# The last token pieces before a layer norm multiplied token tile by token tile, and GpSimd's weight half moved behind the norm's powers

## What is computed

```python
x = layer_norm(ALPHA * x + 0.5 * swiglu(x, ffn1_wg, ffn1_wu, ffn1_wd), ln1_g, ln1_b)
...   # S5, RG-LRU and RWKV-7 branches of x @ w_in, gated and summed into merged
x = layer_norm(ALPHA * x + merged @ mix_w_out, ln2_g, ln2_b)
x = layer_norm(ALPHA * x + cross_attention(x, mem, xa_wq, xa_wkv, xa_wo), ln3_g, ln3_b)
x = layer_norm(ALPHA * x + 0.5 * swiglu(x, ffn2_wg, ffn2_wu, ffn2_wd), ln4_g, ln4_b)

def layer_norm(x, g, b):
    mu = jnp.mean(x, -1, keepdims=True)
    var = jnp.mean(jnp.square(x - mu), -1, keepdims=True)
    return (x - mu) * lax.rsqrt(var + LN_EPS) * g + b
```

## Time and profile before

| what | us |
|---|---|
| median of 3 runs (1621.33 to 1622.28) | 1622.28 |
| the profiled execution, its own time | 1621.9 |
| its span | 1620.1 |
| PE busy | 1572.5 (97%) |
| DVE busy | 1260.5 (78%) |
| ACT busy | 790.0 (49%) |
| POOL busy | 244.8 (15%) |

### The profile page before, as it was taken

The page is one execution under the profiler, slowest core; times in us unless marked ns, Lnnn a source line. Parts: engine busy times, 40 slices in busy tenths (PEclk is TensorE's granted clock), DMA queues, the critical chain, the costliest instruction groups (busy, mean ns, idle before and its releaser), DMA issues.

```text
span 1620.1 us, 31212 instructions
## 1 busy us (share of the span) xinstructions
PE 1572.5 (97%) x13210; PEld 1412.2 (87%) x13210; DVE 1260.5 (78%) x1625; ACT 790.0 (49%) x1003; POOL 244.8 (15%) x176
## 2 busy tenths in 40 slices
PE   8999999999999998999999999999999999999997
PEld 7888889999989987888888888999999999878886
DVE  6799899888558858766688998998885678587666
ACT  4554453663454545444455555346533545454443
POOL 2024520000000402101110435100000004010101
PEclk9999999999999999999999999999999999999999
DMA  8765645443436535566676556554334465456663
GB/s 234 217 188 182 203 138 143 131 125 112 145 117 209 169 136 156 190 190 188 209 188 192 187 181 182 157 141 127 113 110 145 131 209 165 143 156 192 188 192 131
DMA packets 380916, 267.74 MB, mean 165 GB/s; under 512 B 21133, under 2 KB 361577, under 8 KB 380777
## 3 DMA queue, kind: packets, MB, share of 16 engines
q1 hardware_dynamic: 377548, 255.16, 52.0%
q10 hardware_dynamic: 3228, 10.58, 2.0%
HBM read 264.66 MB, written 1.05 MB: 164 GB/s over the span
## 4 chain that ended last, share of the span: by engine, by line
PE 79%; DVE 15%; issue 3%; ACT 2%; ACTq 1%; POOL 0%; DVEq 0%
PE bank L762 17%; PE bank L765 9%; PE bank L735 8%; PE bank L736 8%; PE bank L737 7%; PE banks4to L737 6%; PE banks4to L735 6%; PE banks4to L736 6%; DVE ring_lo L1778 3%; DVE small L1797 1%; DVE x_tok L1792 1%; PE bank L1327 1%; PE bank L1311 1%; PE bank L748 1%; ACT ring_hi L1372 1%
## 5 line engine op out<-in xcount | busy, mean ns | idle before, releaser
L1778 DVE TENSOR_TENSOR ring_lo<-ring_raw,ring_hi 128x1024 fp32r<-128x1024 f32 x466 | 602.2, 1297 | 203.7 <-ACT ring_hi L1372 198.5
L1372 ACT ACTIVATE ring_hi<-ring_raw 128x1024 fp32r<-128x1024 f32 x472 | 497.7, 1058 | 467.6 <-PE bank L765 209.2
L762 PE MATMUL bank<-xT,ring_hi 128*128 128x512 f32 x1344 | 335.6, 392 | 0.0
L762 PEld LDWEIGHTS bank<-xT,ring_hi 128*128 128x128 f32 x1344 | 244.2, 189 | 45.5
L735 PE MATMUL bank<-xT,ring_hi 128*128 128x256 f32 x864 | 251.4, 291 | 3.2 <-DVE ring_lo L1778 2.7
L736 PE MATMUL bank<-xT,ring_hi 128*128 128x256 f32 x864 | 244.6, 283 | 0.9 <-issue 0.9
L737 PE MATMUL bank<-xT,ring_lo 128*128 128x256 f32 x864 | 244.4, 283 | 0.0
L765 PEld LDWEIGHTS bank<-xT,ring_lo 128*128 128x128 f32 x1344 | 183.4, 190 | 13.1
L765 PE MATMUL bank<-xT,ring_lo 128*128 128x256 f32 x1344 | 187.4, 282 | 0.0
L735 PEld LDWEIGHTS bank<-xT,ring_hi 128*128 128x128 f32 x864 | 165.4, 191 | 9.5 <-issue 4.5
L736 PEld LDWEIGHTS bank<-xT,ring_hi 128*128 128x128 f32 x864 | 165.6, 192 | 1.8 <-issue 1.6
(11 more groups left out here) (345 smaller groups left out, 2520.0 us busy)
## 6 DMA issues: line engine op xcount, KB each, us to landing
ring_raw<-in_w_in_dram SPq DMA_DIRECT2D x100, 512.0 KB, 3.8
ring_raw<-in_ffn_wg_dram SPq DMA_DIRECT2D x88, 512.0 KB, 3.8
ring_raw<-in_ffn_wu_dram SPq DMA_DIRECT2D x88, 512.0 KB, 3.8
ring_raw<-in_ffn_wd_dram SPq DMA_DIRECT2D x88, 512.0 KB, 3.5
ring_raw<-in_xa_wkv_dram SPq DMA_DIRECT2D x32, 512.0 KB, 3.9
ring_raw<-in_s_glu_w_dram SPq DMA_DIRECT2D x16, 512.0 KB, 3.3
ring_raw<-in_mix_w_out_dram SPq DMA_DIRECT2D x16, 512.0 KB, 4.3
ring_raw<-in_xa_wq_dram SPq DMA_DIRECT2D x16, 512.0 KB, 4.2
```

The costliest lines, as they stand in the source:

```text
L762: mm(both, hi[:, k, :], xT_both[:, :, k, :], start=(k == 0), stop=(k == ND - 1), skip_group_check=True)
L1372: return nc.scalar.activation(o, i, func, **kw)
L1778: st.mark(tt(lo_flat(n), raw_flat(n), hi_flat(i), ALU.subtract), s_lo["dve"])
```

## The change

There are two edits, one on PE and one on POOL.

On PE, `token_last` takes three pieces for `d0`, `d1` and `wo` instead of two: the second piece of the chunk before is no longer multiplied by `token_piece`. For token tile 0 it goes piece by piece (each piece into both banks of the tile), for tile 1 bank by bank (all three pieces into one, then into the other). The waits for a piece's lo half, for `s_hl` and for `s_oe` now stand where the piece is first used. `s_piece` is raised for all three in the last bank, tile 1 half 1. For `mix` the order of the matmuls stays as it was. On POOL, `piece_lo` in `ln` moves behind the two powers and the bias.

```diff
--- before.py
+++ after.py
@@ -847,21 +847,31 @@
             def by_token(kind, j, src, first, last_chunk):
                 if last_chunk:
                     return token_last(kind, j, src)
-                for m in range(2):
-                    token_piece(kind, j, m, src, first)
+                token_piece(kind, j, 0, src, first)
+                if kind == "mix" or j < NF // 2 - 2:
+                    token_piece(kind, j, 1, src, first)
 
             def token_last(kind, j, src):
 
-                ws = [take(kind, j, m) for m in range(2)]
-                for t in range(NT):
-                    for h in range(2):
-                        for m, w in enumerate(ws):
-                            last = mm3(banks[4 + 2 * t + h][:, :], [x[:, held(kind, j) + m, t * P:(t + 1) * P] for x in src],
-                                       [x[:, 0, 512 * h:512 * (h + 1)] for x in w], False, m == 1)
-                            if t == 1 and h == 1:
-                                last.then_inc(s_piece, 1)
-                            elif m == 1:
-                                last.then_inc(s_acc, 1)
+                parts = [(j, 0), (j, 1)] if kind == "mix" else [(j - 1, 1), (j, 0), (j, 1)]
+                by_piece = [(0, p, h) for p in parts for h in range(2)]
+                by_half = [(1, p, h) for h in range(2) for p in parts]
+                if kind == "mix":
+                    by_piece.sort(key=lambda x: x[2])
+                ws = {}
+                for t, (c, m), h in by_piece + by_half:
+                    if (c, m) not in ws:
+                        if kind[0] == "d" and (c, m) == (j, 0):
+                            pe.wait_ge(*at(s_hl, int(kind[1]) * (NF // 2) + j + 1))
+                        if kind == "wo" and (c, m) == (j, 0):
+                            pe.wait_ge(*at(s_oe, 4))
+                        ws[c, m] = take(kind, c, m)
+                    last = mm3(banks[4 + 2 * t + h][:, :], [x[:, held(kind, c) + m, t * P:(t + 1) * P] for x in src],
+                               [x[:, 0, 512 * h:512 * (h + 1)] for x in ws[c, m]], False, (c, m) == (j, 1))
+                    if (t, h) == (1, 1):
+                        last.then_inc(s_piece, 1)
+                    elif (c, m) == (j, 1):
+                        last.then_inc(s_acc, 1)
 
             def ffn(i):
                 for kind, j in ffn_items(i):
@@ -885,7 +895,8 @@
                     else:
                         if j == 0 and (i or layer[0]):
                             pe.wait_ge(*at(s_lny, 3 * NT * i))
-                        pe.wait_ge(*at(s_hl, i * (NF // 2) + j + 1))
+                        if j < NF // 2 - 1:
+                            pe.wait_ge(*at(s_hl, i * (NF // 2) + j + 1))
                         by_token(kind, j, hT, j == 0, j == NF // 2 - 1)
 
             def ln_turn(n, between=None):
@@ -1355,8 +1366,6 @@
                 values(3)
                 project(1, 1)
                 project(2, 0)
-                project(2, 1)
-                pe.wait_ge(*at(s_oe, 4))
                 token_last("wo", 3, oT)
                 ln_turn(2)
                 ffn(1)
@@ -2491,13 +2500,13 @@
             def ln(n, first=None):
 
                 final = n == 3 and layer[0] == L - 1
-                if first:
-                    piece_lo(*first)
                 for t in range(NT):
                     pool.wait_ge(*at(s_lnv, NT * n + t + 1))
                     st.then(tt(rstd[t], vare[t], NEG_HALF, ALU.pow), s_lnr)
                     if t == 0:
                         st.mark(g.tensor_scalar(nbias[0], mv[0][:, 0:1], rstd[0], -1.0, ALU.mult, ALU.mult), s_lnb)
+                if first:
+                    piece_lo(*first)
                 if final:
                     return
                 for b in range(2):
```

## The result

The changed kernel takes 1631.78 us (median of 4, 1631.43 to 1632.01) against 1622.11 (median of 4) before: ratio 1.0058, interval 1.0046 to 1.0069. It is slower by 9.7 us. The forecast was 1619.0, in a range of 1617.8 to 1621.7. Of the prediction's cases it is rival 1, the slower one, which it had given a chance of 0.07 and priced at 1631.0.

What follows compares the result with a forecast made beforehand. PE was busy 97% of the span, its standstills at layer norms hanging on DVE being late. A gain of 3.5 less 0.2 for the tail gave 3.3: 1622.28 becomes 1619.0 us, whole range 1617.8 to 1621.7.

Steps and rivals of the forecast that it cites:

- rival 1: At five norms POOL's subtraction makes DVE's L1811 wait 2.40 each: 12.0 lost, less 3.3, so 1631.0; chance 0.07.
- DVE's own weight half at s + 5.64: At five norms, DVE's weight half meeting POOL's late subtraction: up to 0.1 a norm, taken as 0.
- s: Moment DVE begins adding the last bank, tile 1 half 1; claimed to fall to 0.04 behind the matmuls' end.
- The gain at the head: DVE's earlier start on the last bank: 0.64 at two `wo` ends, 0.56 at four others, 3.5 us won.
- Tile 0's side: ACT's hi copy and normalising of tile 0: copy ends 0.3 before the matmuls' end, just when wanted; costed at nothing.
- The tail: PE's held-back matmuls want `hidden_lo` 1.39 earlier, giving a new wait: + 0.2 to + 0.35, taken as 0.22.
- rival 3: PE's granted clock falls to half at more norms than two; all five give + 1.5, 1620.5; chance 0.10.

Runs made afterwards that it cites:

- the two halves: Changed kernel with each of POOL's subtractions cut into two of 128 x 512, one behind the other: 1625.32 us against 1622.38 for the kernel before.
- the tail alone: Changed kernel with POOL's subtraction put back ahead of the powers, three-piece tail kept: 1638.98 us against 1622.78 for the kernel before.
- the two-source step: Changed kernel plus a 128 x 1 POOL product of two SBUF sources ahead of the subtraction: 1621.56 us beside 1622.09 before, run once.
- the one-source step: Changed kernel plus a 128 x 1 POOL instruction with one source ahead of the subtraction: 1620.79 us against 1622.38 for the kernel before.
- the version with the wait: Changed kernel with POOL's subtraction made to wait until DVE's L1811 is done: 1620.79 us against 1622.78 for the kernel before.
- the move alone: Kernel before with only POOL's subtraction moved behind the second power, two-piece tail kept: 1634.39 us against 1622.78 before.

## Why the prediction was wrong, step by step

**The failing step** is the one that set rival 1 aside: "Against it: DVE starts L1811 0.04 after the power ends (618.32 + 0.72 against 619.08), while POOL must itself wait for its power's semaphore. Chance 0.07." Because of it the sum has nothing for L1811, where the runs show 2.12 us at each of five norms. The reading was right: DVE was recorded at 620.66 and POOL at 620.70. The inference was not. I took the recorded start for the moment at which an instruction takes the ports, and a lead of 0.04 for a win. It lost five times out of five, and with POOL's subtraction 0.31 behind it won five out of five. With it fell the line "That DVE's own weight half at s + 5.64 meets the tail of POOL's piece can cost up to 0.1 a norm. I take 0; bounds 0 and 0.5": the bound left out the instruction at s + 2.75 that stood right at the place where the piece was put. The Trainium skill (SBUF — State Buffer, "SBUF: two separate sides") says of the pair that whoever starts first gets it for the whole instruction. The trace agrees that the loser stands to the end of the instruction, and the two halves show that it stands no longer. That the recorded start tells who is first is not shown: here the later one by the record had it.

An estimate from the rows fits every outcome. After POOL's instruction ends, a DVE instruction that stood for it needs 0.28 more (0.29 when reckoned from the rounded rows): so L1811 behind the whole subtraction and behind its first half, and so L1806 (0.48 undisturbed) in the version with the subtraction between the powers and in the tail alone. If that last 0.28 is what needs the ports, L1811 needs them from 0.55 - 0.28 = 0.27 behind its recorded start. POOL's subtraction in the run with the two-source step ends 2.21 behind L1820's end, 0.13 less than its undisturbed 2.34, so it needs them from 0.13 on. In the changed kernel POOL's 0.04 + 0.13 = 0.17 comes before DVE's 0.27; with the subtraction at 0.31 it comes after. The two-source step was over 0.24 behind L1820's start, before 0.27, and met nobody; the one-source step would have been over at 0.06 + 0.27 = 0.33, and it stood. No run put the subtraction between 0.04 and 0.31, so where the line lies is estimated and not measured.

**The rival's own price** held in the main: it said 2.4 a norm, the runs say 2.12, since L1811 ends 0.29 behind POOL's instruction and so has part of its own 0.55 behind it by then. That the rival's 1631.0 lies so near the measured 1631.78 is in part luck: L1811 cost 1.4 less than the 12.0 priced, while the clock took 1.5 that the price left out and head and tail together gave 2.7 instead of 3.3.

**The gain at the head** was 3.5 and is 3.1. DVE's start on the last bank lies 0.10 or 0.11 behind the matmuls' end, not 0.04 (617.91 against 617.80), so 0.57 at two ends and 0.50 at four. The rest is as read: first bank at 613.05, 4.75 before the end; tile 1 at 616.34, 1.46 before it; then a pause of 0.16 for PE, which shows that PE and no longer DVE is the later one. In the version with the wait and in the one with the subtraction between the powers s has the same 0.10 or 0.11 at all six.

**Tile 0's side** came as forecast. The hi copy ends just as it is wanted, answering to ACT's part of the earlier trace rows:

```profile
616.45 1.06 ACT L1381 ACTIVATE ring_hi<-ring_raw 128x1024 fp32r<-128x1024 f32 x1 [5.87 <-PE banks4to L737]
...
617.51 1.24 ACT L1381 ACTIVATE x_tok<-x_tok,small 128x1024 f32<-128x1024 f32 x1
```

ACT normalises tile 0 from 617.51, 0.29 before the matmuls' end (forecast 0.3), and PE turned it 0.7 earlier, hidden by tile 1's.

**The tail** was + 0.22 and is about + 0.4. PE before and behind the wait for `hidden_lo`, layer 0 and layer 1, answering to the earlier trace rows:

```profile
193.08 0.40 PE L737 MATMUL banks4to<-ring_hi,hT_lo 128*128 128x512 f32 x1
...
193.71 0.50 PE L735 MATMUL banks4to<-ring_hi,hT_hi 128*128 128x512 f32 x1 [0.22 <-POOL hT_lo L2536]
...
1000.74 0.40 PE L737 MATMUL banks4to<-ring_hi,hT_lo 128*128 128x512 f32 x1
...
1001.04 0.50 PE L735 MATMUL banks4to<-ring_hi,hT_hi 128*128 128x512 f32 x1
```

In layer 0 PE resumes at 193.71, as reckoned, and its last 48 matmuls take 0.21 more than before. In layer 1 I counted only the 0.02 by which the data would be late. They are 0.01 late (there at 1000.98, wanted at 1000.74 + 0.23), and the stop costs more than that: the next matmul starts 0.30 behind, and the one after it 0.34 behind that (1001.38), where the step is 0.23. So 0.18. The other four ends take what they took before.

**The clock** (rival 3) added itself to rival 1, which the prediction had kept apart. In the busy times by stretch (answering to the earlier trace rows; the number after POOL's count is the granted clock) all five norms show it lowered, to the 1.2 GHz level for part or all of the stretch:

```profile
208.00:212.00 4.00, 3.78 (x18) 3.60 (x19) 3.96 (x6) 4.00 (x9) 1.60 (x2) 0.59 0.02 4
...
622.00:626.00 4.00, 2.62 (x11) 2.35 (x12) 3.22 (x6) 1.04 (x3) 1.04 (x1) 0.50 0.33 80
...
816.00:820.00 4.00, 2.75 (x12) 2.48 (x13) 3.22 (x6) 1.18 (x3) 0.91 (x1) 0.54 0.45 130
...
1014.00:1018.00 4.00, 3.99 (x21) 3.62 (x21) 3.67 (x7) 2.92 (x7) 0.00 (x0) 0.57 0.02 4
...
1432.00:1436.00 4.00, 3.91 (x17) 3.64 (x18) 3.22 (x7) 2.33 (x6) 0.00 (x0) 0.50 0.00 0
```

Before it was two. With DVE shut out, PE stood or only turned from 617.80 to 625.25, 7.45 us instead of 5.65. At norm 2 of layer 0, which had kept its clock, that was 13.63 - 10.83 - 2.12 = 0.68 more on top of L1811's 2.12. Part of it is seen in the turning of tile 1, which takes 1.97 there instead of 1.09. In the kernel with the wait two of the five fell, norm 0 of layer 0 and norm 2 of layer 1; where the falls come differs from kernel to kernel, at nearly equal standstills. The mean granted clock of single runs of the kernel before goes from 0.992 to 0.999, so it differs from run to run as well. Treating the falls before as chance was fair; at standstills of over 7 us all five norms fell, in this profile and in that of the move alone.

**The account.** 5 x 2.12 = 10.6 for L1811, less 3.1 at the head, plus 0.4 in the tail, gives 7.9; the span grew by 9.8. Of the other 1.9, 1.5 is what the clock took beyond its cost before. I reckon it to the third matmul of x's low part, since two can run ahead of DVE. At the five norms in their order that matmul starts 0.05, 0.68, 0.68, 0.33 and 0.70 later than s + 10.83 + 2.12, together 2.4; before, the sum above s + 10.83 was 0.9. Of the last 0.4, 0.2 lies between norm 0 and norm 1 of layer 0 and the rest is spread out; I can tie neither to an edit. The head's gain is real and was paid for over three times. One sum of the prediction doesn't come out: the upper bounds that it lists for the forecast (0.36, 0.13, 0.5 and 0.5) added to 1619.0 give 1620.5, not 1620.0. It changes nothing here.

## What to carry to other kernels

Before work is moved on GpSimd to "right after" an instruction whose semaphore VectorE waits for as well, list what VectorE starts at that same moment: two engines released by one event start almost together, and if both want the shared ports, one stands for the other's whole instruction. A long GpSimd instruction belongs where VectorE was seen not to stand for it (here while it added a bank from PSUM and took statistics, 0.69 each with or without, with 0.03 to 0.05 lost on the L1806 behind them: 12 us better than the changed kernel, the best version), or behind VectorE's next step by a wait (11 us better, but it uses up slack that is missed where the clock falls). A head start of a few hundredths of a us in the trace is no evidence of who wins.

## What the hardware showed that I had not expected

- The engine with the earlier recorded start can lose the ports: DVE at 620.66, POOL at 620.70, and DVE ends 0.29 after POOL. With POOL at 0.31 behind, DVE has its 0.55 and POOL takes 0.1 more.
- A DVE instruction of 128 x 512 that stood ends 0.28 us behind POOL's, whether it had stood 2.1 us (L1811), 1.0 (L1811 with the two halves) or 0.03 (L1806).
- A POOL step of 128 x 1 with one source, 0.06 behind DVE, stood (0.53 instead of 0.27), one with two sources, 0.04 behind, did not (0.19), and neither held up DVE. By the estimate above the second was over before DVE needed the ports.
- A wait on PE that was met 0.01 us late cost about 0.18, since two matmuls start 0.30 and 0.34 apart instead of 0.23.
